# GpSimd takes every fourth low-part subtraction of a two-part fp32 kernel, and the bias rows move to the load queue

## The reference, cut to what matters

```python
for l in range(DEPTH):                     # DEPTH = 2
    mod = c_act @ ada_w[l] + ada_b[l]      # a vector times a 2048 x 6144 matrix
    h = rms_norm(x, norm_g[l]) * (1.0 + scale) + shift
    z = h @ w_in[l]                        # q and kv latents, gates, conv inputs
    ...                                    # attention with 8 heads, a 31-tap depthwise conv
    x = x + gate * (concat(mla_out, conv_out) @ w_out[l])
# the second block, once
h = modulate(rms_norm_2(x, g_norm1), sh1, sc1)
qa, ka, va, oa, gates, qb, kb, vb = split(h @ w_in_2)
...                                        # mLSTM on the a parts, window attention on the b parts
s = einsum(qr, kb) * scale + bias          # bias: rpb, gathered by row and column distance
x = x + ga1 * (concat(h_a, h_b) @ w_out_2)
u, g = split(modulate(rms_norm_2(x, g_norm2), sh2, sc2) @ w_up_2)
x = x + ga2 * ((gelu(conv3(g)) * u) @ w_down_2)
```

## Time and profile before

| | |
|---|---|
| three runs | 2579.53, 2583.24, 2583.43 us |
| span of the profiled execution (its own total is not given apart from it) | 2578.3 us |
| median above that span | 4.9 us |
| TensorE busy | 2368.3 us, 92% of the span |
| VectorE busy | 1773.9 us, 69% |
| ScalarE busy | 909.5 us, 35% |
| GpSimd busy | 41.3 us, 2% |
| mean granted TensorE clock | 0.938 |

### The profile page before, as it was taken

How to read it: one execution, slowest core, us unless ns; L and a number is a source line. 1 busy time by engine, 2 the same in 40 slices (tenths; PEclk the granted TensorE clock), 3 DMA queues, 4 the chain that set the end, 5 groups by cost and what they waited for, 6 DMA issues and landing times.

```text
span 2578.3 us, 41885 instructions
## 1 busy us (share of the span) xinstructions
PE 2368.3 (92%) x16533; PEld 2236.9 (87%) x16533; DVE 1773.9 (69%) x2368; ACT 909.5 (35%) x1330; POOL 41.3 (2%) x57
## 2 busy tenths in 40 slices
PE   2289999899899998998998999988999999999998
PEld 2189998779899987798997999768999999999998
DVE  6777798776777988668959583577876656654443
ACT  1053322323543223234333341135544444433333
POOL 0000000000000000005000000000000000000000
PEclk7588899899988999999999998989999999999999
DMA  8869654776596647677968794236865555555552
GB/s 302 316 213 333 237 172 145 247 231 226 198 333 241 183 141 255 204 246 225 348 203 274 255 363 149 74 123 200 273 219 182 184 179 184 182 165 184 180 184 94
DMA packets 413234, 557.41 MB, mean 216 GB/s; under 512 B 25139, under 2 KB 362103, under 8 KB 412868
## 3 DMA queue, kind: packets, MB, share of 16 engines
q1 hardware_dynamic: 409536, 550.70, 64.9%
q0 software_dynamic: 1120, 2.18, 0.5%
q10 hardware_dynamic: 2468, 3.07, 0.3%
HBM read 553.72 MB, written 2.17 MB: 216 GB/s over the span
## 4 chain that ended last, share of the span: by engine, by line
PE 79%; DVE 12%; DMA 4%; issue 2%; ACT 2%; DVEq 0%; ACTq 0%; SPq 0%
PE gemm L1346 70%; DVE ada_acc L913 4%; DMA ada_raw<-in_ada_w 3%; PE stat L1365 2%; PE stat L1373 1%; DVE w_lo L940 1%; DVE scr L968 1%; DVE h_lo L973 1%; PE bankS L1490 1%; PE bankO L1395 1%; PE bankS L1489 1%; ACT w_hi L667 1%; DVE ss L1111 1%; PE stat L1357 0%; ACT h_full L703 0%
## 5 line engine op out<-in xcount | busy, mean ns | idle before, releaser
L940 DVE TENSOR_TENSOR w_lo<-w_raw,w_hi 128x1024 fp32r<-128x1024 f32 (+1 forms) x564 | 669.7, 1198 | 441.3 <-ACT w_hi L667 439.0
L1346 PE MATMUL gemm<-h_hi,w_hi 128*128 128x256 f32 x3136 | 905.0, 289 | 45.5 <-DVE h_lo L973 19.9
L1346 PE MATMUL gemm<-h_lo,w_hi 128*128 128x256 f32 x3136 | 899.8, 287 | 0.0
L1346 PE MATMUL gemm<-h_hi,w_lo 128*128 128x256 f32 x3136 | 899.3, 287 | 0.0
L667 ACT ACTIVATE w_hi<-w_raw 128x1024 fp32r<-128x1024 f32 (+1 forms) x564 | 571.6, 1028 | 751.7 <-PE gemm L1346 631.1
L1346 PEld LDWEIGHTS gemm<-h_hi,w_hi 128*128 128x128 f32 x3136 | 615.9, 196 | 48.9 <-issue 33.7
L1346 PEld LDWEIGHTS gemm<-h_lo,w_hi 128*128 128x128 f32 x3136 | 615.6, 196 | 0.4
L1346 PEld LDWEIGHTS gemm<-h_hi,w_lo 128*128 128x128 f32 x3136 | 614.8, 196 | 0.0
L913 DVE SCALAR_TENSOR_TENSOR ada_acc<-ada_raw,c_act,ada_acc 128x1024 f32<-128x1024 f32 x360 | 460.1, 1295 | 33.0 <-DMA ada_raw<-in_ada_w 29.6
L1346 PE MATMUL gemm<-G_hi,w_hi 128*128 128x256 f32 x704 | 200.1, 284 | 3.1 <-DVE w_lo L940 3.1
L1346 PE MATMUL gemm<-G_lo,w_hi 128*128 128x256 f32 x704 | 199.9, 284 | 0.0
(11 more groups left out here) (267 smaller groups left out, 2613.3 us busy)
## 6 DMA issues: line engine op xcount, KB each, us to landing
w_raw<-in_w_in SPq DMA_DIRECT2D x264, 512.0 KB, 5.6
ada_raw<-in_ada_w SPq DMA_DIRECT2D x192, 512.0 KB, 5.3
w_raw<-in_w_up SPq DMA_DIRECT2D x176, 512.0 KB, 3.5
ada_raw<-in_w_ada SPq DMA_DIRECT2D x168, 512.0 KB, 5.2
w_raw<-in_w_out SPq DMA_DIRECT2D x96, 512.0 KB, 5.3
w_raw<-in_w_down SPq DMA_DIRECT2D x64, 512.0 KB, 3.6
ada_late<-in_w_ada SPq DMA_DIRECT2D x24, 512.0 KB, 4.3
w_raw<-in_w_down SPq DMA_DIRECT2D x32, 384.0 KB, 3.6
```

What stands on the lines that cost most here:

```text
L940: dve.tensor_tensor(w_lo[:, fixed % PARTS, 0:sz], w_raw[:, fixed % RAW, 0:sz], w_hi[:, fixed % PARTS, 0:sz].bitcast(F32), ALU.subtract).th ...
L1346: last = pe.matmul(half(g, k, q), left, right, start=(kt == 0 and j == 0), stop=(u == len(g.units) - 1 and t == nk - 1 and j == len(parts) ...
```

## The change

A unit whose place in the ring of four is 3 (`POOL_UNIT`) gets its low part on GpSimd; VectorE leaves it out and goes on with what stands beside it. There are two semaphores for the low parts, `w_split` and `w_split_pool`, and TensorE waits for the one that belongs to the unit. GpSimd's old work is put between products: the table `rpb_pad` is filled at the start, `lower` is made ahead of `qb`, one half of the bias is masked after `qb` and the other after `kb`. The 32 bias loads move to SyncE's queue, ahead of the loads of the sixth of eight blocks of the second layer's `outm`.

```diff
+        POOL_UNIT = 3
+        def on_pool(fixed):
+            return fixed % PARTS == POOL_UNIT
+        def wait_split(e, g, i, k, u):
+            per, fixed = g.body * len(g.units), g.unit(0, k, u)[1]
+            s = fixed - g.unsplit
+            if on_pool(fixed):
+                e.wait_ge(w_split_pool, i * (per // PARTS) + (s // PARTS + 1))
+            else:
+                e.wait_ge(w_split, i * (per // PARTS * (PARTS - 1)) + (s // PARTS * (PARTS - 1) + s % PARTS + 1))
...
+            def bias_load():
+                sp.wait_ge(pad_stored, 32)
+                sp.wait_ge(o_read, NH * LAYERS)
+                for r in range(ROWS):
+                    g0 = GRID * (r % 2)
+                    for h in range(NH):
+                        src = bass.AP(rpb_pad.tensor, (h * (2 * WIN_ROWS - 1) + WIN_ROWS - 1 - r) * PAD,
+                                      [[1, GRID], [PAD, ROWS], [1, GRID]])
+                        sp.dma_start(bias[g0:g0 + GRID, r // 2, h], src).then_inc(bias_loaded, 16)
...
+                if g is G["outm", LAYERS - 1] and isinstance(i, int) and (i, k) == (1, 1):
+                    bias_load()
...
-            wait_out(pool, G["outm", LAYERS - 1])
...
+            def prep(g, i, k, before=None, beside=None, done=None):
+                for u, (k0, nk) in enumerate(g.units):
+                    n, fixed = g.unit(i, k, u)
+                    if g.native or not on_pool(fixed):
+                        continue
+                    pool.wait_ge(w_hi_done, n + 1 - g.unsplit)
+                    sz = nk * g.cols
+                    pool.tensor_tensor(w_lo[:, fixed % PARTS, 0:sz], w_raw[:, fixed % RAW, 0:sz],
+                                       w_hi[:, fixed % PARTS, 0:sz].bitcast(F32), ALU.subtract).then_inc(w_split_pool, 1)
...
+            for g in prods:
+                if g is G["qb"]:
+                    break
+                ahead(pool, g, prep, none)
+            link(pool.memset(lower[:], 0.0))
...
+            ahead(pool, G["qb"], prep, none)
             pool.wait_ge(bias_loaded, 16 * ROWS * NH)
...
-            for g0 in range(0, P, GRID):
+            for g0, done in ((0, G["qb"]), (GRID, G["kb"])):
+                pool_split_done(done)
...
+                pool.wait_ge(bias_masked, g0 // GRID + 1)
+                ahead(pool, G["kb" if g0 == 0 else "vb"], prep, none)
+            for name in ("qa", "ka", "va", "oa", "mg"):
+                ahead(pool, G[name], prep, none)
             wait_out(pool, G["mg"])
+            pool_split_done(G["mg"])
...
+            for name in ("out2b", "out2a", "upa", "upb", "down"):
+                ahead(pool, G[name], prep, none)
...
@@ VectorE's prep
-                    if not g.native:
+                    if not g.native and not on_pool(fixed):
                         dve.wait_ge(w_hi_done, n + 1 - g.unsplit)
...
@@ TensorE's multiply
-                            pe.wait_ge(w_split, n + 1 - g.unsplit)
+                            wait_split(pe, g, i, k, u)
```

More of the change, by code:

```diff
@@ L220, in program @@
         w_split = sem("w_split")
+        w_split_pool = sem("w_split_pool")
         w_used = sem("w_used")
@@ L557, in _ @@
             ins.then_inc(mask_done, 1)
-            wait_out(pool, G["outm", LAYERS - 1])
-            link(pool.memset(lower[:], 0.0))
-            for t in range(TT):
-                ins = pool.affine_select(out=lower[:, t, :], in_=lower[:, t, :], compare_op=ALU.is_ge,
-                                         fill=FAR, base=-P * t, pattern=[[1, T]], channel_multiplier=-1)
-            ins.then_inc(mask_done, 1)
             nrow = NH * (2 * WIN_ROWS - 1)
@@ L573, in _, with pool_split_done @@
                            a["rpb_2"][0].rearrange("h r c -> (h r) c")).then_inc(pad_stored, 16)
[L574 to L581, removed]
+            def prep(g, i, k, before=None, beside=None, done=None):
[7 more added lines that the diff above has]
+                                       w_hi[:, fixed % PARTS, 0:sz].bitcast(F32), ALU.subtract).then_inc(w_split_pool, 1)
+            def pool_split_done(g):
+                follower = after[id(g)]
+                ahead_units = 0 if follower.native or len(follower.units) > PARTS else len(follower.units)
+                pool.wait_ge(w_split_pool, (g.u0 + g.blocks * len(g.units) + ahead_units - g.unsplit) // PARTS)
+            pool.wait_ge(mask_done, 1)
+            prep(prods[0], 0, 0)
+            for g in prods:
[3 more added lines that the diff above has]
+            link(pool.memset(lower[:], 0.0))
+            for t in range(TT):
+                ins = pool.affine_select(out=lower[:, t, :], in_=lower[:, t, :], compare_op=ALU.is_ge,
+                                         fill=FAR, base=-P * t, pattern=[[1, T]], channel_multiplier=-1)
+            ins.then_inc(mask_done, 1)
+            ahead(pool, G["qb"], prep, none)
             pool.wait_ge(bias_loaded, 16 * ROWS * NH)
@@ L603, in _ @@
             pool.memset(one_row[:], 1.0).then_inc(sel_done, 1)
+            pool.wait_ge(sel_done, 1)
+            for name in ("out2b", "out2a", "upa", "upb", "down"):
+                ahead(pool, G[name], prep, none)
         @block.scalar
```

## The result

The changed kernel takes 2588.55 us (median of 12 runs, 2584.31 to 2593.73) where the kernel before takes 2581.07 us beside it on the same chip: a ratio of 1.0033, with a 95% interval of 1.0020 to 1.0045. It is slower by a third of a per cent. I had forecast 2575.2 us, a gain; the sign was wrong. The profiled execution took 2591.48 us, 2.9 above the median, so the two traces differ by more (11.3 us of span) than the medians do (7.5).

What follows compares the result with a forecast made beforehand. TensorE, busy 92% of the span, was taken as the bound, so work off VectorE pays only where TensorE waits for it. The terms summed to -8.0 us, 2583.2 to 2575.2 us, range 2565 to 2600.

Steps and rivals of the forecast that it cites:

- the price of SyncE's issues: In outm: 32 bias-load issues at 0.43 us take 13.8 us; unit 10's load is late but covered, 0.
- Rival 3: In outm: SyncE issues of 0.64 us stall it 5.7 us, then the clock 2.5: 2583.4 us; chance 0.10.
- Sum after `upa`: At the sum after upa: GpSimd's 2.2 us operation takes the lock where a 1.14 us subtraction stood, +0.9 us.
- its even blocks: Even blocks, read in upb and applied to upa: GpSimd has 3.3 us for an operation of 2.2, so 0.
- Convolution: Beside gate: VectorE is full, the moved subtractions cost it time, 0.3 us of cover is missing, twice: +0.6 us.
- They take turns, one operation each: Wherever GpSimd and VectorE both read two SBUF operands: they alternate; a moved subtraction costs VectorE up to 2.2 us.
- the term -7.0: At the sum after ua: 1.9 us idle for 3.6 and faster small matmuls, 3.5 us, twice: -7.0 us.
- The masks' leaving `qb`: In qb: the 4.70 us of idle time and the half clock after it go, -7.2 us.
- The masks beside `kb`: Beside kb: two masks take turns with VectorE, so the third subtraction behind them is late, +1.2 us.
- Behind the norms: Behind the norm of each layer: GpSimd's operation delays the third unit's subtraction, +1.0 us each, +2.0 us together.
- `qa` to `mg`: Attention beside qa: four subtractions leave VectorE, but each new operation holds it 1.5 us; +1.5 us, between -2 and +4.
- rival 2: At two norms and kb: new gaps bring the half clock, +7.5 us, 2582.7 us, no change; chance 0.22.

Runs made afterwards that it cites:

- e1: The changed kernel with its 32 bias loads issued three at a time behind outm's weight loads, not in one burst: 2582.54 us, ratio 1.0018.
- e2: The changed kernel with every subtraction back on VectorE, the burst of bias loads and the moved masks kept: 2577.19 us, ratio 0.9997 to the kernel before.
- e5: e1 with all subtractions of the product upa back on VectorE: 2577.17 us, ratio 0.9989 to the kernel before.
- e6: e1 with all subtractions of the product gate back on VectorE: 2578.51 us, ratio 1.0001 to the kernel before.

## Why the prediction was wrong

**The step that failed first is the price of SyncE's issues.** I wrote "32 issues at 0.43 us are 13.8 us" and took **0**. 0.43 us was the row of one weight load on that queue, although the bias loads' own row, on GpSimd's queue, said 0.64. It took 0.67: the same transfer costs about the same on either queue, and another transfer's row was the wrong one to take. Rival 3 had the mechanism and the price (5.7 us and 2.5 for the clock; measured 5.43 and 2.4), at a chance of 0.10: with 0.64 in hand for the same transfer it should have been the likeliest case. e1 and e2 show that it is the burst: with GpSimd's share gone (e2) the loss stays, with the loads spread (e1) it goes. It is 8.3 of the stage's 9.9 us.

**Sum after `upa`, and its even blocks.** Predicted +0.9 and 0; the stage has +6.8 and e5 gives it back. I took the cover of an even block (3.3 us) from a row of `upb` and said it for `upa` too. In `upb` it was right, no subtraction there is ever waited for. In `upa` ScalarE's table load takes 1.28 us of that cover, leaving about 2.0 for 2.4. Ahead of the sum there was 1.8 us more idle time than before, twice what I allowed, and the gap of 1.20 us in the norm ahead of `upa` stood in no term.

**Convolution.** Predicted +0.6 by a VectorE that loses its turns. In the changed kernel's second layer that is what happened: the two rows of steps shown above became 2.2 and 2.1 us longer, and TensorE did not wait. In the first layer, and in both layers of e1 and e5, VectorE lost nothing in the long row: its steps ran on at 0.40 us and GpSimd starved. So the cost came on the other engine: TensorE waited for GpSimd's low part, +4.1 us in one layer of the changed kernel (2.6 of idle time, 1.7 at low clock), and 2.9 us in each of the two layers between e1 and e6. "They take turns, one operation each" was drawn from masks beside pieces of 1.2 us and does not always hold for a row of short steps.

**Right:** the operation's length (2.41 us, predicted 2.2; a VectorE row beside it took 3.4 us as predicted). The idle time ahead of the sums, 1.93 and 1.92 us. Their small matmuls took 5.94 and 5.01 us (5.18 expected), so the term -7.0 came out at -6.4: 1.7 idle and 1.1 clock in layer 1, 1.7 and 2.0 in layer 2. The masks' leaving `qb`: no idle time, full clock. The masks beside `kb`: a gap of 1.33 us for 1.2. Behind the norms there was one gap of 0.81 us for two of 1.0. `qa` to `mg` has +2.3 for +1.5, which is luck: by the end of the attention beside `qa` it is +0.9, and the rest comes from stretches behind it that have no idle time and differ in the clock (0.51 from 1478 to 1484 us, where before it was full), some longer and some shorter.

The three missed terms are 8.3, 5.9 and about 3.8 us beyond what I allowed, 18.0 together; -8.0 and 18.0 are +10.0, where the spans of the two traces differ by +11.3 and the medians by +7.5. That it is so near is partly luck, since entries of both signs that I can't ascribe to the change cancel in the rest of the table.

**What stays open.** The clock behind short gaps. The same 1.9 us of idle time ahead of the sum gave a mean clock of 0.60 in one layer and 0.72 in the other; the same gap of 2.6 us in `gate` was followed by 0.66 in the changed kernel and by 1.00 in e1 and e5; and the 2 us that `ub` gains at its start in some traces come with 3.60 us of idle time ahead of the sum (e2) as well as with 1.9. No run separates what decides it. Nor was tried what decides whether GpSimd gets its turn in a row of 0.4 us steps or waits for the row's end.

## What to carry to other kernels

Work moved to an idle engine is priced where the result is needed, not where the time is freed: VectorE lost 55 us of work and TensorE, the bound, gained only where that work stood ahead of a result it was waiting for, and there a change of order gave the same. Price a DMA issue by a row of the same transfer, and never put a burst of small ones ahead of loads with a few us of cover; spread them. A cover measured in one loop is to be read again in every loop that looks like it: here one more table load on a third engine used it up.

## What was unexpected of the hardware

- Between VectorE's steps of two SBUF operands and 0.40 us, back to back, GpSimd's subtraction often did not advance: 10.03 us for 2.41, five times in three traces at the same step (once in the changed kernel, in both layers of e1 and e5), while the steps themselves kept their length. The sixth time (second layer of the changed kernel) it got in first, took 2.78 us, and one step was held to 2.6 us instead. The Trainium skill (SBUF — State Buffer, Who interferes with whom) describes the pair that the two engines share, and says that whoever issues first keeps it for the whole instruction. The traces agree for single instructions, and add that a row of instructions can keep the other side out for 8 us. The section also says that `tensor_scalar` in a two-port mode can take the pair. Here one was held beside GpSimd (the 2.76 us above), which no row of before showed. Beside operations of 1.2 us both sides were held, once each (VectorE's 1.2 became 3.4).
- The issue of a bias load (64 KB) took 0.64 us on GpSimd's queue and 0.67 on SyncE's, against 0.43 for a 512 KB weight load by itself; between bias loads a weight load's issue took 0.44 to 0.61.
- The gaps of 2.62 and 5.43 us in a run of products were followed by 27 and 24 matmuls at a mean clock of 0.66 and 0.50, which added 1.7 and 2.4 us. But gaps of 2.61 to 2.63 us at the same place in e1 and e5, four in all, were followed by full clock. The gap of 1.33 us beside `kb` added nothing to its own length, so rival 2 did not come true there.
